# S5 mixer: u ahead of slots and second rotation table, Toeplitz rows first in SyncE's turn, two GLU products ahead of the last block's outputs

## The reference

```
u = rmsnorm(h, mix_norm_w[1])                      # 512 x 1024, 64 groups of 16 channels
for d in (forward, backward):                      # 64 complex states for each group
    lb = exp((a_re + i a_im) * exp(log_step));  q = (lb - 1) / (a_re + i a_im)
    state[t] = lb * state[t-1] + q * (b @ u[t])    # backward: t+1
    y += Re(c @ state)
y = y + d_skip * u;  g = gelu(y);  hh = g @ w_glu + b_glu
h = h + hh[:, :1024] * sigmoid(hh[:, 1024:])
```

## Time and profile before

| what | us |
|---|---|
| median of 3 runs | 1607.53 (1607.35 to 1607.68) |
| the profiled execution | 1606.47 |
| its span, first to last instruction | 1604.8 |
| S5 mixer, first drive to first GLU product | 951.2 to 1070.2 |

### The profile page before, as it was taken

One profiled execution on the slowest core, in us unless ns is written; L12 is line 12 of the kernel. 1 busy time (PEld: TensorE's weight loads), 2 busy tenths in 40 slices (PEclk: granted clock), 3 DMA queues, 4 the chain that ended last, 5 costly groups with the idle time before them and its releaser, 6 DMA issues.

```text
span 1604.8 us, 20223 instructions
## 1 busy us (share of the span) xinstructions
PE 1524.5 (95%) x7365; PEld 1239.3 (77%) x7365; DVE 1189.6 (74%) x1371; ACT 718.6 (45%) x1091; POOL 243.8 (15%) x244
## 2 busy tenths in 40 slices
PE   7988999999989999999999989999999999999996
PEld 6757777687667888888876769988888888888884
DVE  5687768678787989988898969955677666643356
ACT  4554454444644555134445342433365555532242
POOL 1154111020127400030075100000100000000000
PEclk9999999999999999999999976979999999999998
DMA  4334215144225334543436587932233333332221
GB/s 141 86 122 132 79 66 173 51 145 131 66 66 108 115 119 143 196 133 130 151 118 209 174 299 249 264 85 94 93 95 99 94 93 103 105 98 92 92 92 59
DMA packets 192234, 199.01 MB, mean 124 GB/s; under 512 B 47886, under 2 KB 178526, under 8 KB 188062
## 3 DMA queue, kind: packets, MB, share of 16 engines
q1 hardware_dynamic: 184510, 192.76, 37.8%
q10 hardware_dynamic: 7648, 5.25, 1.2%
HBM read 169.47 MB, written 28.51 MB: 123 GB/s over the span
## 4 chain that ended last, share of the span: by engine, by line
PE 74%; DVE 15%; issue 5%; DMA 3%; ACT 2%; SPq 1%; POOL 0%; DVEq 0%; ACTq 0%
PE ring L2093 21%; PE ring L2083 21%; PE ring L2084 21%; DVE w_lo L1462 2%; PE ring L2349 2%; PE pe_s L2369 2%; DVE cc L1584 1%; PE ring L2234 1%; PE pe_s L2359 1%; DMA w_raw<-in_ssd_w_out 1%; DVE ytmp L1758 1%; DVE zs L1764 1%; DVE fwd L1622 1%; PE pe_s L2104 1%; DVE rstd L1486 1%
## 5 line engine op out<-in xcount | busy, mean ns | idle before, releaser
L2083 PE MATMUL ring<-uh,w_hi 128*128 128x512 f32 x1160 | 459.4, 396 | 10.5 <-DVE cc L1584 3.7
L2084 PE MATMUL ring<-ul,w_hi 128*128 128x512 f32 x1160 | 454.5, 392 | 0.0
L1045 ACT ACTIVATE w_hi<-w_raw 128x1024 fp32r<-128x1024 f32 (+1 forms) x233 | 239.5, 1028 | 437.5 <-PE ring L2084 348.4
L1462 DVE TENSOR_TENSOR w_lo<-w_raw,w_hi 128x1024 fp32r<-128x1024 f32 (+1 forms) x233 | 287.7, 1235 | 162.1 <-PE ring L2093 143.9
L2093 PE MATMUL ring<-uh,w_lo 128*128 128x512 f32 x1160 | 289.1, 391 | 6.3 <-DVE w_lo L1462 6.2
L2083 PEld LDWEIGHTS ring<-uh,w_hi 128*128 128x128 f32 x1160 | 219.5, 189 | 63.1 <-issue 10.9
L2093 PEld LDWEIGHTS ring<-uh,w_lo 128*128 128x128 f32 x1160 | 218.2, 188 | 53.5 <-DVE w_lo L1462 7.5
L2084 PEld LDWEIGHTS ring<-ul,w_hi 128*128 128x128 f32 x1160 | 219.4, 189 | 47.5 <-issue 1.7
L2083 PE MATMUL ring<-gh,w_hi 128*128 128x512 f32 x480 | 189.0, 394 | 4.0 <-ACT w_hi L1045 2.7
L2084 PE MATMUL ring<-gl,w_hi 128*128 128x512 f32 x480 | 188.1, 392 | 0.0
L1971 DVE SCALAR_TENSOR_TENSOR cc<-cin,par,cc 128x512 f32<-128x512 f32 x176 | 129.5, 796 | 1.0 <-ACT cc L1396 1.0
(11 more groups left out here) (329 smaller groups left out, 2050.9 us busy)
## 6 DMA issues: line engine op xcount, KB each, us to landing
w_raw<-in_ffn_w_up SPq DMA_DIRECT2D x88, 512.0 KB, 3.5
w_raw<-in_ffn_w_down SPq DMA_DIRECT2D x40, 512.0 KB, 3.4
w_raw<-in_ssd_w_in SPq DMA_DIRECT2D x32, 512.0 KB, 4.2
s_tables<-tab SPq DMA_DIRECT2D x16, 1024.0 KB, 4.9
slot<-s_tables SPq DMA_DIRECT2D x16, 1024.0 KB, 7.8
fwd<-log_decays SPq DMA_DIRECT2D x16, 512.0 KB, 5.0
w_raw<-in_ssd_w_out SPq DMA_DIRECT2D x16, 512.0 KB, 3.5
w_raw<-in_ple_w_gate SPq DMA_DIRECT2D x16, 512.0 KB, 3.4
```

The source lines that it names most:

```text
L1045: act.activation(w_hi[u % 2][:, 0:n], w_raw[:, u % 2, 0:n], ACT.Copy).then_inc(hi_done, 1)
L1462: dve.tensor_tensor(w_lo[u % 2][:, 0:n], w_raw[:, u % 2, 0:n], w_hi[u % 2][:, 0:n].bitcast(F32), ALU.subtract).then_inc(lo_done, 1)
L2083: pe.matmul(o, wh[:, k, c], rh[:, k0 + k, :], start=first and k == 0, stop=False)
L2084: mm_ = pe.matmul(o, wh[:, k, c], rl[:, k0 + k, :], start=False, stop=False)
```

## The change

- **SyncE's start of S5.** The loads of slot (2, 1) and of rotation table 1 stood ahead of the saves of u. The rotation table now goes behind the lifts of u 0 and 1, the slot behind `toeplitz_load(0)`. `v_out(2)` on ACT goes behind `bq_mask(2)`, and on PE `v_transposes(2)` goes from before drive(0) to behind drive(1).
- **SyncE's turn.** In pass b it issues u_lift(b + 4), toeplitz_load(b + 2), the two slots of b + 4, and then the read-back of block b - 1 (`y_load`). For blocks 0 to 5 ACT issues all eight saves of y. Blocks 6 and 7 are saved by both engines as before.
- **Two GLU products.** In pass 7 the GLU units 0 and 1 are multiplied between within5(7) and outputs5(7). The first six low parts of g are made by GpSimd. ACT and DVE split the weights of GLU unit 2 earlier, and the split of g goes before `y_out(6)`.
- **kernel0** uses a numbered ring tile (`k0`), which is still bank 3, and so the GLU tiles begin at bank 0.

```diff
@@ Plan
             if layer == 1:
+                tile("k0", 1)
                 tile("glu", 16, True)
@@ sync
+            def y_load(b):
+                sp.wait_ge(y5_saved[b % 2], 16 * LC * (b // 2 + 1))
+                if b >= 2:
+                    sp.wait_ge(y5_gelu, b - 1)
+                sp.dma_start(y5[:, b % 2, :], y_dram[b].rearrange("g c t k -> (g c) (t k)")
+                             ).then_inc(y5_in[b % 2], 16)
...
                 rotation_load(0)
                 slot_load(2, 0)
-                slot_load(2, 1)
-                rotation_load(1)
                 u_save(0)
                 u_save(1)
                 u_lift(0)
                 u_lift(1)
-                sp.wait_ge(k0_evac, 1)
+                rotation_load(1)
+                sp.wait_ge(evac, T["k0"] + 1)
...
                 u_save(2)
+                toeplitz_load(0)
+                slot_load(2, 1)
+                u_lift(2)
                 slot_load(3, 0)
-                toeplitz_load(0)
-                u_lift(2)
...
                 for b in range(NB):
                     if b + 4 < NB:
                         u_lift(b + 4)
+                    if b + 2 < NB:
+                        toeplitz_load(b + 2)
+                    if b + 4 < NB:
                         slot_load(b + 4, 0)
                         slot_load(b + 4, 1)
-                    sp.wait_ge(y5_evac, b + 1)
-                    (four saves of y, toeplitz_load(b + 2), read-back of y b)
+                    if 0 < b < NB - 2:
+                        y_load(b - 1)
+                    if b >= NB - 2:
+                        (wait for y5_evac, four saves of y)
+                        if b == NB - 2:
+                            y_load(b - 1)
+                        y_load(b)
@@ gpsimd
+            pool.wait_ge(y5_full, NB - 2)
+            for m in range(KD - 2):
+                pool.wait_ge(g5_hi, m + 1)
+                pool.tensor_tensor(gl5[:, m, :], u5[:, m, :], gh5[:, m, :].bitcast(F32), ALU.subtract).then_inc(g5_lo, 1)
@@ scalar
-                        for t in range(LC // 2):
+                        for t in range(LC if b < NB - 2 else LC // 2):
...
-                    v_out(2)
                     decay_row(1)
                     bq_mask(2)
+                    v_out(2)
...
-                        if b == NB - 1:
-                            for m in range(4, NB - 2):
-                                g5_split(m)
-                        if b + 2 < NB:
-                            rotation_load(b + 2)
-                        y_out(b)
                         if b == NB - 2:
                             act.wait_ge(y5_full, NB - 3)
                             for m in range(4):
                                 g5_split(m)
+                        if b == NB - 1:
+                            for m in range(4, NB - 2):
+                                g5_split(m)
+                            hi_to(U["glu"] + 2)
+                        if b + 2 < NB:
+                            rotation_load(b + 2)
+                        y_out(b)
@@ vector
-                    dve.wait_ge(y5_full, NB - 2)
-                    for m in range(KD):
+                    lo_to(U["glu"] + 2)
+                    dve.wait_ge(g5_lo, KD - 2)
+                    for m in range(KD - 2, KD):
                         g5_rest(m)
@@ tensor
-                    v_transposes(2)
                     drive(0)
...
                         if b == 0:
+                            v_transposes(2)
                             kernels(2)
                         within5(b)
+                        if b == NB - 1:
+                            pe.wait_ge(z_done, 2 * NB - 2)
+                            pe.wait_ge(g5_lo, 4)
+                            product(u, t, 4, 0, gh5, gl5, last=False)
+                            pe.wait_ge(z_done, 2 * NB)
+                            product(u + 1, t + 2, 4, 0, gh5, gl5, last=False)
...
                         outputs5(b)
-                    pe.wait_ge(z_done, 2 * NB)
...
+                            if i == 0 and kg == 0:
+                                continue
                             if i == 0:
-                                pe.wait_ge(g5_lo, 4 * kg + 4)
+                                pe.wait_ge(g5_lo, KD)
```

More of the change, by code:

```diff
@@ L689, in s5_loads @@
                         u_lift(b + 4)
+                    if b + 2 < NB:
+                        toeplitz_load(b + 2)
+                    if b + 4 < NB:
                         slot_load(b + 4, 0)
                         slot_load(b + 4, 1)
-                    sp.wait_ge(y5_evac, b + 1)
[L693 to L696, removed]
-                    if b + 2 < NB:
[L698 to L703, removed]
+                    if 0 < b < NB - 2:
+                        y_load(b - 1)
+                    if b >= NB - 2:
+                        sp.wait_ge(y5_evac, b + 1)
+                        for t in range(LC // 2, LC):
+                            sp.dma_start(y_dram[b, :, :, t, :].rearrange("g c k -> c g k"),
+                                         gy[S5H * t:S5H * t + S5H, b % 2, :].rearrange("p (g k) -> p g k", g=GB)
+                                         ).then_inc(y5_saved[b % 2], 16)
+                        if b == NB - 2:
+                            y_load(b - 1)
+                        y_load(b)
             for layer, parts in enumerate(PARTS):
@@ L1907, in _ @@
                         if m == 1:
-                            pair = bank(3)[:, 0:32 * NB].rearrange("p (b half q) -> p b half q", b=NB, half=2)
+                            pair = bank(T["k0"])[:, 0:32 * NB].rearrange("p (b half q) -> p b half q", b=NB, half=2)
                             dve.wait_ge(stage_ready, 5)
-                            dve.wait_ge(k0_full, 1)
+                            dve.wait_ge(filled, FILL["k0"] + 1)
                             dve.scalar_tensor_tensor(out=d_diag, in0=pair[:, :, 0, :], scalar=halves[:, 0:1], in1=d_diag,
@@ L2331, in kernel0 @@
                                 for a in range(2):
-                                    mm_ = pe.matmul(bank(3)[32 * i:32 * i + 32, 32 * b:32 * b + 32],
+                                    mm_ = pe.matmul(bank(T["k0"])[32 * i:32 * i + 32, 32 * b:32 * b + 32],
                                                     bq[:, a, gs, :].rearrange("p g h -> p (g h)"),
@@ L2335, in kernel0 @@
                                                     start=(b, a) == (0, 0), stop=a == 1, skip_group_check=True)
-                        mm_.then_inc(k0_full, 1)
+                        mm_.then_inc(filled, 1)
                     def drive(b):
@@ L2344, in drive @@
                         if b == 1:
-                            pe.wait_ge(k0_evac, 1)
+                            pe.wait_ge(evac, T["k0"] + 1)
                         for a in range(2):
@@ L2371, in outputs5 @@
                         mm_.then_inc(y5_full, 1)
-                    pe.wait_ge(evac, T["glu"])
+                    pe.wait_ge(evac, T["k0"])
                     kernels(0)
@@ L2378, in _ @@
                     v_transposes(1)
-                    v_transposes(2)
                     drive(0)
                     pe.wait_ge(var_done, 3)
+                    u, t = U["glu"], T["glu"]
                     for b in range(NB):
```

6 lines of the change are left out of this document (2 added, 4 removed).

## The result

| what | us |
|---|---|
| before, median of 5 runs | 1607.53 (1604.58 to 1608.59) |
| after, median of 5 runs | 1616.11 (1614.30 to 1631.92) |
| ratio of the two, 95% interval | 1.0073 (1.0041 to 1.0105) |
| the profiled execution of after, its span | 1631.92, 1630.2 |

The ratio makes the changed kernel slower by 0.73%, which is 11.7 us of 1607.53; it is not the quotient of the two medians, which lie 8.6 us apart. The forecast was 1605.4 in a range of 1600.5 to 1610.5. The profiled execution of after is 15.8 us above its own median, so its trace tells the mechanisms, and the ratios tell their sizes.

What follows compares the result with a forecast made beforehand. In the mixer of layer 1, TensorE and VectorE were taken to bound in turns. A gain of 8.6 us up to block 7 and a loss of 6.5 at the end gave -2.1: 1605.4 us, range 1600.5 to 1610.5.

Steps and rivals of the forecast that it cites:

- part 2: Blocks 0 to 7: DVE starts one every 12.55 us without waits; block 7 starts 8.6 us earlier, at 1042.9.
- a rival with a chance of 0.15: Middle blocks: y read behind the slots holds ACT's gelu and rotation loads; DVE waits 6.9 us, +4.8, 1612.3; chance 0.15.
- Toeplitz first: SyncE's turn: rows ahead of the slots remove PE's 2.39 us hole, the half clock to 1044 and the late drive(7).
- Part 1: Start of S5: 1.5 MB moved behind the lifts of u starts drive(0) 2.8 us earlier, bounds 0 and 4.4.
- The clock: PE: half clock in the drives, full from about 967, so drive(2) is in time; bounds 1.5 us loss or no wait.
- the front gains more: Rival, start: the clock holds through the shorter wait, drive(0) takes 3.6 us not 6.7; -5.2, 1602.3; chance 0.25.
- ACT's four extra issues: Blocks 0 to 5: 1.78 us per four, covered by ACT's 5.21 us wait, so no cost; uncovered 10.7 us of ACT.
- Part 3: End: two products ahead of outputs5(7) uncover its 8.7 us chain; the third product starts later, a loss of 6.5 us.
- the bounds of 1.6 and 6.5: End: loss from the product order, 1.6 us all at the full clock, 6.5 us with the half clock counted.
- the fast bound: End, all at full clock: third product 33.4 us after S, the start of DVE's block 7, a loss of 1.6.
- S + 38.3: End: third product starts 38.3 us after DVE's block 7 starts (S), against 31.8 before, with the half clock counted.

Runs made afterwards that it cites:

- Part 2 alone: Kernel before with only SyncE's turn in the new order (y read back one block late, behind the slots) and ACT issuing all eight saves of blocks 0 to 5: 1.0061.
- the second execution of after: The changed kernel, unedited, run and profiled once more: ratio 1.0082 to before, profiled execution 1619.12 us, median 1620.21 us.
- the read-first run: Kernel before with the new SyncE turn and ACT's eight saves, but the read-back of y of block b - 1 ahead of the two slots: 1.0012.
- the run in which ACT was on time: Kernel before with the new start, slot (2, 1) ahead of Toeplitz rows 0, and ACT issuing all eight saves of blocks 0 to 5: 0.9987.
- the whole change with the read first: The changed kernel with the read-back of y of block b - 1 moved ahead of the two slots: 1.0018 to before.
- parts 1 and 2 together: The changed kernel without the two early GLU products, so new start and new SyncE turn on the kernel before, run twice: 1.0008 and 1.0015.
- part 1 alone: Kernel before with only the new start: u ahead of slot (2, 1) and rotation table 1, transposes of block 2 behind drive(1): 0.9982.
- all four kernels with part 1 and without part 2: Kernel before with the new start: as it is (0.9982), slot (2, 1) first (0.9980), that with ACT's eight saves (0.9987), or that slot order with one product ahead (0.9978).
- part 3 alone: Kernel before with only two GLU products ahead of outputs5(7), six subtractions on GpSimd, the moved splits and tile k0: 1.0021.

## Why the prediction was wrong

**The step that failed** is in part 2: the read-back of y behind the slots entered the sum at nothing and was left to a rival with a chance of 0.15. The forecast had DVE run eight blocks without a wait, a gain of 8.6 us up to block 7. Part 2 alone costs 0.61%, 9.8 us, and moving only the read takes back 0.49% of it, or 0.55 to 0.64% in the whole change. In the second execution of after block 7 starts 0.6 us earlier against R than before, not 8.6. The rival's mechanism held: it had the read issued about 7 us into the turn and landed some 15, measured were 7.3 and 15.4 in one turn (and over 10 us to the issue in the two behind it), with DVE waiting for tables at blocks 4, 5 and 6. Its time, 1612.3, came nearer than the forecast, with too low a price: it counted only the table, at 2.3 us in each of three blocks. Behind the same gelu stand the emptying of `pe_s` and the copies of the transposed tables, and holes of 2.5 and 3.3 us on PE, behind these, were each followed by a stretch at the half clock. The argument held against the rival, that SyncE is quiet just then, did not hold: SyncE waited 17.5 us for saves of kernels ahead of the Toeplitz rows. The 2 MB ahead of the read counted most, since the read-first run keeps 12.4 us of that wait and still regains most of the loss. The Trainium skill (DMA: Bandwidth & Descriptors, "Issuing engines are not separate DMA queues") has the transfers of all issuers run on the same DMA engines. No run here tests that between issuers, since the slots and the read are both SyncE's; among SyncE's own the order of issue moved the median landing between 3.4 and 8.8 us.

**Toeplitz first** was right in that its 2.39 us hole went, and wrong in its worth. By itself it costs 0.36%, and in its trace the slots come late in place of the rows. The prediction looked at the transfer that gained and not at the 2 MB that it was moved past.

**Part 1** held, and was somewhat undersized: drive(0) came 3.7 us earlier and not 2.8, and the ratio gives 0.18%, 2.9 us. The wait for slot (2, 1) was not foreseen, but the slot's place proved to be worth nothing measurable. The reason can be read from the traces: in the profile of after the drives ran at the full clock, PE was ready for kernels(2) at R + 19.2, and the slot came at R + 23.8. In the second execution, with the same order of loads, PE came to kernels(2) only at R + 25.3.

**The clock.** The forecast had the half clock in both drives and the full one from about 967. In the profile of after the clock was 1.00 in the drives and fell to 0.50 in the hole before kernels(2), so both halves of that step failed in this execution, and the drives ran as the rival "the front gains more" had it. In the second one the drives took 12.64 us for 64 matmuls, nothing waited ahead of kernels(2), and blocks 1, 2 and 3 started every 12.5 us. There the step held. The prediction also put the fall of the clock into the hole before drive(0). Windows of 1 us of the kernel before show it behind the start of the drive at 951.22:

```profile
951.00:952.00 1.00, 0.78 (x6) 0.81 (x7) 0.00 (x0) 0.97 (x3) 0.00 (x0) 0.87 1.19 225
952.00:953.00 1.00, 1.00 (x7) 1.00 (x6) 0.00 (x0) 0.20 (x1) 0.00 (x0) 0.50 1.39 301
```

The hole ahead of the drive was longer in the profile of after (2.06 us) than before (1.45 us), and there the clock held. So a short hole did not decide this, and what did stays open.

**ACT's four extra issues** were priced at nothing. That fits the run in which ACT was on time. Behind a late gelu the eight issues took 5.57 us, and PE's hole of 2.20 us and the half clock ahead of block 7 followed. No run has the late read with ACT's four saves only, so their share is open.

**Part 3** was right in its mechanism: the chain that outputs5(7) leaves uncovered was put at 8.7 us and measured 8.67 to 8.98. Its size was not one number. Alone it costs 0.21%, 3.4 us, between the bounds of 1.6 and 6.5; the whole change with the read first has S + 33.4, the number of the fast bound, though not its course: within5(7) took 3.65 us there, the half clock. With the late reads it costs 0.6 to 0.7%, about 10 us, since the splits and GpSimd's subtractions come late as well. That they would be hidden was wrong there: the first product waited 4.14 us for them. That the third product then started at S + 37.8, beside S + 38.3 in the forecast, is luck: the forecast had the half clock there and no such wait, and the trace has outputs5(6) and within5(7) at the full clock (3.74 and 1.97 us) and the wait.

**Adding up.** 0.61 - 0.18 would be 0.43% for parts 1 and 2 together, and 0.08 and 0.15% were measured. The traces show two things that fit, neither tested by itself. In both traces of these two parts DVE's first four blocks start every 12.5 us, where part 2 alone lost 1.0 and 3.2 us at blocks 2 and 3 (the kernel before, 0.9 and 2.0). And part 1 alone has Toeplitz waits of 8.8 us in total, one of them 5.25 us at within5(2), which part 2 takes away. Whether these account for all of it stays open: the trace of after has 21 us more than before from R to the third product, the ratio gives 11.7, so single traces can't close such a sum. It is also open why the Toeplitz rows of block 2 land 4.0 to 6.3 us late in all four kernels with part 1 and without part 2.

## What to carry to other kernels

A small read that is put behind bulk transfers in one list has to be priced by everything that stands in order behind its consumer, not by the one tile that is wanted next. A move in a full queue has two sides: ask for each transfer that it passes when that one is wanted. And work that is pulled ahead to fill a wait is taken from wherever it gave cover before; on the kernel before, one product ahead cost nothing measurable and the second 0.23 to 0.29%; behind late reads even one cost some 0.4%.

## What was not expected of the hardware

- The clock fell during gapless work. In the kernel before it was granted at 1.00 up to the first matmuls of the drives and at 0.50 from 952 on, with PE busy 100%; in the second execution of after it was 1.00 at 953 to 954 and 0.50 from 955. The 64 matmuls then took 13.41 and 12.64 us. In the first execution of after the same 64 took 7.33 us, at 1.00 throughout.
- GpSimd's 128x512 subtractions took 2.1 us each on the mean in the second execution of after, where they ran beside DVE's scans of block 7. In part 3 alone the first four, which began 0.5 us ahead of that block and not 3.0 us behind its start, took 1.4 us each. DVE's last rotations, 1.22 us when undisturbed, took 2.12 and 2.30 us beside them. The timeline of DVE in the second execution of after:

```profile
1068.74 2.12 DVE L1892 TENSOR_TENSOR ct<-rb,erot 128x1024 f32<-128x1024 f32 x1
1070.79 2.30 DVE L1893 TENSOR_TENSOR ct<-rb,erot 128x1024 f32<-128x1024 f32 x1
```

- The traces reach R between 937.84 and 944.51 us; kernels whose edits all lie behind R do so at 943.25 (part 2 alone) and 937.84 (before). A difference of a few us between two single profiles is no evidence until it is counted from a common event.
